# PEER expert values: half of V read densely through a one-hot coefficient matrix, half gathered and added on VectorE

## What is computed

```python
def peer(x, w_q, sub_keys, u_tab, v_tab):
    ...
    def block_fn(args):
        xb, eb, gb = args
        u = u_tab[eb]
        h = jnp.einsum("thkd,td->thk", u, xb)
        coef = gb * jax.nn.gelu(h, approximate=False)
        return jnp.einsum("thk,thkd->td", coef, v_tab[eb])
```

## Time and profile before

| what | value |
|---|---|
| median of 3 runs (lowest to highest) | 3728.76 us (3727.88 to 3730.0) |
| the profiled execution, its own time | 3730.43 us |
| its span, first to last instruction | 3728.6 us |
| mean granted TensorE clock | 0.892 of 2.4 GHz |
| busy: PE, DVE, POOL, ACT | 3077, 2145, 1871, 588 us |
| moved by DMA | 1240.58 MB, mean 333 GB/s |
| of these by gathers | 1073.81 MB, 69.4% of the DMA engines' time |

### The profile page before, as it was taken

How to read it: one execution, slowest core, us unless ns; L and a number is a source line. 1 busy time by engine, 2 the same in 40 slices (tenths; PEclk the granted TensorE clock), 3 DMA queues, 4 the chain that set the end, 5 groups by cost and what they waited for, 6 DMA issues and landing times.

```text
span 3728.6 us, 33147 instructions
## 1 busy us (share of the span) xinstructions
PE 3077.4 (83%) x10013; PEld 1755.1 (47%) x10013; DVE 2145.3 (58%) x3196; ACT 587.7 (16%) x1043; POOL 1871.0 (50%) x1448
## 2 busy tenths in 40 slices
PE   8968896888788878788799998958878887887887
PEld 7855792333333333333397977923333333333333
...
GB/s 240 141 84 65 139 164 353 422 422 422 422 422 421 422 422 422 422 419 422 365 194 183 135 124 144 167 349 422 422 422 422 422 422 422 422 422 422 422 422 339
DMA packets 256836, 1240.58 MB, mean 333 GB/s; under 512 B 17861, under 2 KB 116741, under 8 KB 118277
## 3 DMA queue, kind: packets, MB, share of 16 engines
q0 software_dynamic: 147456, 1073.81, 69.4%
...
...
## 4 chain that ended last, share of the span: by engine, by line
PE 41%; DMA 33%; DVE 12%; issue 7%; POOL 6%; ACT 1%; POOLq 0%; DVEq 0%; SPq 0%; ACTq 0%
DMA ring<-in_peer_v,index_now 33%; PE ps L629 23%; PE ps L491 8%; PE ps L511 7%; DVE work L900 6%; POOL ring L452 3%; POOL ring L460 1%; POOL index_now L444 1%; PE ps L555 1%; DVE x_tok L988 1%; PE ps L528 1%; DVE work L1052 0%; DVE work L1049 0%; DVE work L998 0%; DVE work L1007 0%
## 5 line engine op out<-in xcount | busy, mean ns | idle before, releaser
L629 PE MATMUL ps<-ring,diag 128*128 128x512 f32 x4096 | 2057.5, 666 | 522.5 <-DMA ring<-in_peer_v,index_now 462.7
L1111 DVE SCALAR_TENSOR_TENSOR ring<-ring,x_tok 128x2048 f32<-128x2048 f32 x512 | 1176.6, 2299 | 1115.2 <-DMA ring<-in_peer_u,index_now 1114.0
L629 PEld LDWEIGHTS ps<-ring,diag 128*128 128x128 f32 x4096 | 867.0, 215 | 1713.0 <-issue 1147.9
L460 POOL DMA_INDIRECT ring<-in_peer_v,index_now x512 | 808.6, 1579 | 812.7 <-PE ps L629 735.8
L452 POOL DMA_INDIRECT ring<-in_peer_u,index_now x512 | 512.7, 1001 | 291.3 <-issue 128.2
L426 POOL TENSOR_TENSOR w_lo<-ring,w_hi 128x2048 fp32r<-128x2048 f32 x34 | 159.8, 4703 | 657.2 <-ACT w_hi L716 657.2
L800 ACT ACTIVATE gelu_now<-h_now 128x1 f32<-128x1 f32 x512 | 103.8, 203 | 2291.3 <-DVE ring L1111 2291.3
L953 DVE TENSOR_TENSOR w_lo<-ring,w_hi 128x2048 fp32r<-128x2048 f32 x78 | 178.8, 2292 | 265.5 <-ACT w_hi L716 265.5
L491 PE MATMUL ps<-x_hi,w_hi 128*128 128x256 f32 x1024 | 292.0, 285 | 16.5 <-DVE x_lo L1077 7.2
L491 PE MATMUL ps<-x_lo,w_hi 128*128 128x256 f32 x1024 | 289.5, 283 | 0.0
L491 PE MATMUL ps<-x_hi,w_lo 128*128 128x256 f32 x1024 | 286.6, 280 | 0.0
...
## 6 DMA issues: line engine op xcount, KB each, us to landing
...
ring<-in_peer_u,index_now POOLq DMA_INDIRECT x512, 10.3
ring<-in_peer_v,index_now POOLq DMA_INDIRECT x512, 11.7
```

Of the source, the lines that this page charges most:

```text
L460: pool.indirect_dma_start(row_tile(1, s), None, v_tab, bass.IndirectOffsetOnAxis(ap=index_now[:, half, s:s + 1], axis=0)).then_inc(v_row[s ...
L629: mm = pe.matmul(ps[:, Q * tb + q, :], diag[:, s, :], row_tile(1, s)[:, q * 512:(q + 1) * 512], start=False, stop=True, skip_group_check=True)
L1111: dve.scalar_tensor_tensor(out=row_tile(0, s), in0=row_tile(0, s), scalar=1.0, in1=x_tok[:, tb, :], op0=ALU.mult, op1=ALU.mult, accum_out= ...
```

## The change

U tiles are still gathered whole, now into a ring of eight, and VectorE's dots write straight into `coef`. The Gelu and the gates are applied once per block. V is split by columns. Columns 0 to 1023 are gathered (4 KB per row, `v_tab` is viewed as half rows, `index_v` counts those) and added by VectorE, `x_tok += coef * row`, in place. Columns 1024 to 2047 of all 16384 experts are read in order, 128 tiles of 128 experts, and TensorE multiplies each with a matrix `mix[tb]` that holds, for every token and every expert, the coefficient or zero.

`mix` is built from one-hot masks. For each token VectorE compares a row of 0 to 127 with key1 and with key2 of its slots (`masks`, four tokens in one instruction), ScalarE scales the first mask by the coefficients (`weigh_hot`), TensorE multiplies the two (`mix_slots`), which sums over slots, and ScalarE copies the product into `mix` (`take_mix`). The first block's batches are spread among the second block's dots; the second block's matrix lies in the ring and is built when the dots are done. Both norms come at the end. The norm's rows lie where the dense tiles land (`all_v`), so SP loads them late.

```diff
--- before, GpSimd
-pool.indirect_dma_start(
-    row_tile(0, s), None, u_tab,
-    bass.IndirectOffsetOnAxis(ap=index_now[:, half, s:s + 1], axis=0)).then_inc(u_row[s], 16)
-pool.wait_ge(v_used, i * (2 * RING) + ((base + half) * RING + s + 1))
-pool.sem_inc(pool_tick, 1)
-pool.indirect_dma_start(
-    row_tile(1, s), None, v_tab,
-    bass.IndirectOffsetOnAxis(ap=index_now[:, half, s:s + 1], axis=0)).then_inc(v_row[s], 16)
+++ after, GpSimd: eight U gathers per copy of indices, then, behind all of them, the half rows
+for s in range(U_RING):
+    if opening and half == 0 and s == RING:
+        pool.wait_ge(proj, 2 * (P_WQ[layer] + PANELS))
+    pool.wait_ge(u_used, i * (2 * U_RING) + ((base + half) * U_RING + s + 1))
+    pool.sem_inc(pool_tick, 1)
+    pool.indirect_dma_start(
+        u_tile(s), None, u_tab,
+        bass.IndirectOffsetOnAxis(ap=index_now[:, half, s:s + 1], axis=0)).then_inc(u_row[s], 16)
...
+def gather_adds(half, first_slot, count, copies, n):
+    pool.tensor_copy(index_add[:, half, :, 0:count], index_v[:, :, first_slot]).then_inc(index_copied, 1)
+    pool.wait_ge(index_copied, copies)
+    pool.sem_inc(pool_tick, 1)
+    for k in range(TB * count):
+        pool.wait_ge(g_used, n + k)
+        pool.sem_inc(pool_tick, 1)
+        pool.indirect_dma_start(
+            add_tile(k), None, v_tab,
+            bass.IndirectOffsetOnAxis(ap=index_add[:, half, k % TB, k // TB:k // TB + 1], axis=0)).then_inc(g_row[k], 16)
--- before, SP
-load_rows(1)
-sp.wait_ge(u_used, RING + TB * SLOTS)
+++ after, SP
+def load_v(layer):
+    rows = peer_v[layer]
+    full = NKEY // D_RING - 1
+    sp.wait_ge(ln_steps[2 * layer], TB * LN_STEPS)
+    with sp.Fori(0, full) as i:
+        for k in range(D_RING):
+            sp.wait_ge(d_used, i * D_RING + (layer * NKEY + k + 1))
+            sp.dma_start(all_v[:, k, :], rows[bass.ds(i * (D_RING * P) + k * P, P), HALF:D]).then_inc(v_all[k], 16)
+    sp.wait_ge(mix_taken, 2 + BATCHES * TB * (layer + 1))
+    for k in range(D_RING):
+        row = full * D_RING + k
+        if k == 2:
+            sp.wait_ge(d_used, D_RING + layer * NKEY + full * D_RING)
+            load_rows(2 * layer + 1)
+        if k >= 2:
+            sp.wait_ge(d_used, D_RING + layer * NKEY + row - 1)
+        sp.dma_start(last_v[:, k % 2, :], rows[row * P:(row + 1) * P, HALF:D]).then_inc(v_last[k % 2], 16)
+load_v(0)
+sp.wait_ge(d_used, D_RING + NKEY)
--- before, TensorE
-for tb in range(TB):
-    for q in range(Q):
-        residual(tb, q)
-    base = (layer * TB + tb) * GROUPS
-    with pe.Fori(0, GROUPS) as i:
-        for s in range(RING):
-            pe.wait_ge(diag_done, i * RING + (base * RING + s + 1))
-            pe.wait_ge(v_row[s], i * 16 + (base + 1) * 16)
-            for q in range(Q):
-                mm = pe.matmul(ps[:, Q * tb + q, :], diag[:, s, :], row_tile(1, s)[:, q * 512:(q + 1) * 512],
-                               start=False, stop=True, skip_group_check=True)
-            mm.then_inc(v_used, 1)
+++ after, TensorE
+def turn_slots(tb):
+    pe.wait_ge(route[layer], part_at(tb, 1) + PART_INDEX)
+    n = layer * TB + tb
+    if n:
+        pe.wait_ge(slot_taken, n)
+    for c in range(2):
+        pe.transpose(ps[:, 2, c * P:(c + 1) * P], row_e[:, tb, c, :], ident[:, :])
+    pe.wait_ge(coef_done, n + 1)
+    pe.transpose(ps[:, 2, 2 * P:3 * P], coef[:, tb, :], ident[:, :]).then_inc(slot_ready, 1)
+def mix_slots(tb):
+    at = (layer * TB + tb) * BATCHES
+    with pe.Fori(0, BATCHES // 2) as i:
+        for b in range(2):
+            pe.wait_ge(hot_ready, i * 2 + (at + b + 1))
+            pe.wait_ge(mix_taken, i * 2 + (at + b + 1))
+            for k in range(BATCH):
+                mm = pe.matmul(ps[:, b, k * P:(k + 1) * P], hot_2[:, b, k, :], hot_1[:, b, k, :], start=True, stop=True)
+            mm.then_inc(mix_ready, 1)
+for tb in range(TB):
+    turn_slots(tb)
+    mix_slots(tb)
+for tb in range(TB):
+    for q in range(Q // 2, Q):
+        pe.matmul(ps[:, dense_bank(tb, q), :], alpha_ident[:, :], x_tok[:, tb, q * 512:(q + 1) * 512],
+                  start=True, stop=True, skip_group_check=True)
+def weigh(row, tile):
+    for tb in range(TB):
+        for q in range(Q // 2, Q):
+            mm = pe.matmul(ps[:, dense_bank(tb, q), :], mix[tb][:, row, :], tile[:, q * 512 - HALF:(q + 1) * 512 - HALF],
+                           start=False, stop=True, skip_group_check=True)
+    return mm
+full = NKEY // D_RING - 1
+pe.wait_ge(mix_taken, 2 + BATCHES * TB * (layer + 1))
+for i in range(full):
+    for k in range(D_RING):
+        pe.wait_ge(v_all[k], (layer * full + i + 1) * 16)
+        weigh(i * D_RING + k, all_v[:, k, :]).then_inc(d_used, 1)
+for k in range(D_RING):
+    pe.wait_ge(v_last[k % 2], (2 * layer + k // 2 + 1) * 16)
+    mm = weigh(full * D_RING + k, last_v[:, k % 2, :]).then_inc(d_used, 1)
--- before, ScalarE
-act.activation(gelu_now[:, s:s + 1], h_now[:, s:s + 1], ACT.Gelu).then_inc(gelu_done, 1)
+++ after, ScalarE (written twice, for tb 0 and 1)
+def take_slots(tb):
+    n = layer * TB + tb
+    act.wait_ge(u_used, U_RING + (n + 1) * SLOTS)
+    act.activation(coef[:, tb, :], coef[:, tb, :], ACT.Gelu).then_inc(gelu_done, 1)
+    act.wait_ge(slot_ready, n + 1)
+    act.activation(by_slot[:, tb, :, :], ps[:, 2, 0:3 * P].rearrange("p (a b) -> p a b", a=3), ACT.Copy) \
+       .then_inc(slot_taken, 1)
+def take_mix(tb, i, b):
+    at = (layer * TB + tb) * BATCHES
+    act.wait_ge(mix_ready, i * 2 + (at + b + 1))
+    act.activation(mix[tb][:, :, bass.ds(i * (2 * BATCH) + b * BATCH, BATCH)],
+                   ps[:, b, :].rearrange("p (k a) -> p a k", k=BATCH), ACT.Copy).then_inc(mix_taken, 1)
+def weigh_hot(tb, i, b):
+    for k in range(BATCH):
+        last = act.activation(hot_1[:, b, k, :], hot_1[:, b, k, :], ACT.Copy,
+                              scale=by_slot[:, tb, 2, bass.ds(i * (2 * BATCH) + (b * BATCH + k), 1)])
+    last.then_inc(hot_ready, 1)
...
+take_slots(0)
+act.wait_ge(slot_taken, layer * TB + 1)
+made = layer * TB * 2 * BATCHES
+with act.Fori(0, BATCHES // 2) as i:
+    for b in range(2):
+        act.wait_ge(hot_made, i * 4 + (made + 2 * b + 2))
+        weigh_hot(0, i, b)
+        if b:
+            take_mix(0, i, 0)
+    take_mix(0, i, 1)
--- before, VectorE
-route_part(layer, 0, 1)
-for tb in range(TB):
-    for half in range(2):
-        dots(tb, half, 0 if half else 1, GROUPS // 2)
-        if tb == 0:
-            route_part(layer, 1, half)
-    if tb == 0:
-        dots(1, 0, 0, 1)
-    norm(2 * layer + 1, tb, lambda q: mixer_sum(tb, q))
+++ after, VectorE
+def dot(tb, s, landed_at, slot):
+    dve.wait_ge(u_row[s], landed_at)
+    dve.scalar_tensor_tensor(out=u_tile(s), in0=u_tile(s), scalar=1.0, in1=x_tok[:, tb, :],
+                             op0=ALU.mult, op1=ALU.mult, accum_out=coef[:, tb, slot]).then_inc(u_used, 1)
...
+def weights(tb):
+    dve.wait_ge(gelu_done, layer * TB + tb + 1)
+    dve.tensor_tensor(out=coef[:, tb, :], in0=coef[:, tb, :], in1=gate[:, tb, :], op=ALU.mult).then_inc(coef_done, 1)
+def add(k, tb, n, slot):
+    dve.wait_ge(g_row[k], n[0])
+    dve.wait_ge(g_used, n[1])
+    dve.scalar_tensor_tensor(out=x_tok[:, tb, 0:HALF], in0=add_tile(k), scalar=coef[:, tb, slot], in1=x_tok[:, tb, 0:HALF],
+                             op0=ALU.mult, op1=ALU.add).then_inc(g_used, 1)
+def masks(tb, b):
+    if layer or tb or b:
+        dve.wait_ge(mix_ready, (layer * TB + tb) * BATCHES + b - 1)
+    for c, hot_c in enumerate((hot_1, hot_2)):
+        dve.tensor_tensor(out=hot_c[:, b % 2, :, :], in0=iota_f[:, :].unsqueeze(1).to_broadcast([P, BATCH, P]),
+                          in1=by_slot[:, tb, c, b * BATCH:(b + 1) * BATCH].unsqueeze(2).to_broadcast([P, BATCH, P]),
+                          op=ALU.is_equal).then_inc(hot_made, 1)
+for h in range(PH):
+    if h == EARLY_HEADS:
+        route_part(layer, 0, 0)
+    if h == PH - 1:
+        opening_dots(0, RING)
+    route_head(layer, h)
+route_part(layer, 0, 1)
+opening_dots(RING, U_RING)
+dots(0, 1, GROUPS // 2)
+route_part(layer, 1, 0)
+dots(0, GROUPS // 2, GROUPS)
+route_part(layer, 1, 1)
+dots(1, 0, 1)
+weights(0)
+dots(1, 1, 2)
+dve.wait_ge(slot_taken, layer * TB + 1)
+for b in range(BATCHES):
+    masks(0, b)
+    if b < 28 and b % 2:
+        dots(1, 2 + b // 2, 3 + b // 2)
+weights(1)
+for tb in range(TB):
+    dve.tensor_scalar(x_tok[:, tb, 0:HALF], x_tok[:, tb, 0:HALF], ALPHA, None, ALU.mult).then_inc(x_scaled, 1)
+uses = [-(-(TILES - k) // G_RING) for k in range(G_RING)]
+dve.wait_ge(slot_taken, layer * TB + 2)
+dve.wait_ge(x_scaled, (layer + 1) * TB)
+for b in range(BATCHES):
+    masks(1, b)
+    if b % 2:
+        n = b // 2
+        add(n % G_RING, n % TB, ((layer * uses[n % G_RING] + n // G_RING + 1) * 16, G_RING + layer * TILES + n - 1),
+            slice(n // TB, n // TB + 1))
+with dve.Fori(0, (TILES - FIRST_ADDS) // G_RING) as i:
+    for m in range(G_RING):
+        n = FIRST_ADDS + m
+        k = n % G_RING
```

(44 more changed lines are left out.)

201 lines of the change are left out of this document (119 added, 82 removed).

## The result

The changed kernel takes 3706.93 us (median of 4 runs, 3700.73 to 3710.15), the kernel before 3729.31 beside it: ratio 0.9938, 95% interval 0.9924 to 0.9953. That is 22 us faster, where 81 were forecast. The range held the time and the direction was right; the gain was a quarter of what the sum said. The profiled execution took 3707.39 us, its span 3705.7 (before: 3728.6).

A forecast was written before the change was run, and what follows sets the result against it. Full DMA engines, gathering U and V tiles at 422 GB/s, were taken to bound the kernel. Four stages per layer save 42 us, 83 for both; 3730.4 - 83 is 3647, given as 3648, range 3590 to 3800 (8 in 10).

The forecast's parts named there:

- the sum: Four stages in a row make a layer of 1249 us, 42 less than before, 83 for both layers.
- A: U gathers and dots: 665 us, to 1235; GpSimd's turns as fast as the DMA, plus 7 us for taking turns.
- They tie: First token block's dots: VectorE with routing needs 323 us, to 893, and the DMA 288, to 890.
- B: Second block's coefficient matrix, built after the last dot: 83 us, with 8 for the handover and 8 for the end.
- I take 2.1, nearer the floor: Second block's 32 mask batches: 2.1 us each, 67 us in all, near VectorE's floor of 1.84.
- the chain of 2.9: Ceiling per mask batch with two buffers: masks, ScalarE's weighings, matmuls and eviction in a row, 5.8 us for two.
- Rival 2: Second block's matrix is long: 3.4 us a batch, 42 us more, total 3732; chance 0.14.
- This is the price of the change: While the second block's matrix is built, the DMA engines are nearly idle.
- C: Dense V matmuls beside gathered adds: DMA binds at 1.29 us a half tile, 462 us plus 20 of tail, 482.
- Rivals 1, 3 and 4: Gather issues cost two adds, 3844, chance 0.11; dense rows starve, 3932, 0.07; quicker tiles and matrix, 3578, 0.10.
- Rival 1: GpSimd's gather issues miss gaps between VectorE's adds: 2.4 us a gather, 98 us more a layer, total 3844; chance 0.11.
- D: Both norms stand at the layer's end: 17 us, 19 with their waits.

The follow-up runs named there:

- u_no_copy: The changed kernel, but GpSimd takes each U gather's index column from the whole index tile and no longer copies eight columns ahead: 3679.76 us.
- b_order: The changed kernel, but in the second block's matrices ScalarE weighs the next batch before it evicts the present one: 3688.30 us.
- b_four_buffers: As b_order, with four buffers of masks instead of two for the second block, and gathered adds starting only behind the last matrix: 3676.47 us.
- b_adds_34: The changed kernel, but 34 gathered adds instead of 16 stand among the masks of the second block: 3655.80 us.

## Why the prediction was wrong in its size

A layer came out 25 and 29 us longer than the sum, and 8 us came from outside the layers. By steps:

- **A, "9 x 2.21/8 = 2.49 us a tile, as fast as the DMA, no faster", failed.** A turn of GpSimd is as long as the distance of the dots, and that is 2.49 us when they wait for tiles. Nine turns for eight tiles are 9 x 2.49/8 = 2.80 us, slower than the DMA's 2.485, so the ring runs down; measured were 2.76 and 2.91. I had allowed 7 us; u_no_copy shows 15 and 20.
- **"They tie" at 893 failed.** The first block with both parts of the routing took 355.6 us to the second block's first dot, not 323. With the copies gone it is still 340.4: 12 tiles were there by 602, as forecast, but the last of the 128 lands at 900 and not at 890, its dot ends at 902, and the second part, 10 us, stands behind that instead of beside it. Some of it came back: from there to the last dot 317.5 us, 327 forecast, as tiles had gathered in the ring.
- **B, "I take 2.1, nearer the floor", failed.** The batches took 88.5/32 = 2.77 us, near the chain of 2.9 that I had worked out and then discounted. b_order and b_four_buffers show it: with the order changed 2.4, with four buffers and the clock that came with them 1.9, VectorE's floor. Rival 2 had the right place at the wrong price: the strided eviction took 0.60 us, 0.62 forecast, and TensorE's eight records 1.16 to 2.08, 1.0 to 1.7 forecast; two buffers and ScalarE's order put them in a row. The handover and the end were 1.8 and 2.5 us where I had put 8 and 8, so B as a whole was only 10 late.
- **"This is the price of the change" failed**, though no number hung on it: b_adds_34 shows that the idle DMA engines in B could be used for 4 us.
- **C was right, by its reason.** 480 us for 482; DMA share 1.02 at 405 GB/s, which is 0.524/0.405 = 1.29 us a half tile, as on the line between the packets of the earlier trace rows. TensorE worked 440.9 of 448 us at full clock, 30 us ahead of the last add (20 to 40 forecast); gather issues took 1.32 and 1.43 us on average, under 2. The reason given for the tail, gathers alone at one per 1.5 us, held in layer 1 only (the last adds 1.58 us apart on average, DMA share 0.83); in layer 0 layer 1's weights were read beside them, the share stayed at 1.02 and the adds stood 1.89 us apart. Rivals 1, 3 and 4 did not come. Rival 1's mechanism is real, but it bound in A.
- **D and the rest.** Two norms took 16.2 us, 19 forecast. The norm ahead of the slots was priced at nothing; 4.2 us a layer went there, 4.2 of the 6.7 between the layers. I don't know what makes the other 2.5: it drifts in and out over the attention, in steps of under 1 us.

Two slips of the working weigh nothing: the median of 3728.8 less 83 is 3646 and not 3648, and the 0.89 us of rival 1 run from the next dot's start, not from the first one's end.
